# Two gate-quarter loads and a weight split change places at the start of a four-stage transformer kernel

## The reference

```
sh_m, sc_m, gt_m, sh_f, sc_f, gt_f = split(silu(c) @ ada_w[0] + ada_b[0], 6)
h  = rms_norm(x, norm_g[0, 0]) * (1 + sc_m) + sh_m
y  = pool_mixer(h, pool_w, pool_scale)          # 4 groups of 256 columns, windows 2, 4, 8, 16
x  = x + gt_m * rms_norm(y, norm_g[0, 1])       # the "new x"
hf = rms_norm(x, norm_g[0, 2]) * (1 + sc_f) + sh_f
x  = x + gt_f * rms_norm(square(relu(hf @ ffn_w1[0])) @ ffn_w2[0], norm_g[0, 3])
```

## Time and profile before

| | |
|---|---|
| Runs | 972.87, 975.52, 980.09 us |
| Profiled execution | 980.94 us, span 978.9 us |
| TensorE (PE), matmul | busy 957.6 us, 98% of the span |
| VectorE (DVE) | 533.5 us, 54% |
| ScalarE (ACT) | 333.8 us, 34% |
| GpSimd (POOL) | 36.2 us, 4% |
| Chain that ended last | 94% PE, 2% DVE, 2% DMA, 1% ACT |
| Granted TensorE clock, mean | 0.989 of full speed |

### The profile page before, as it was taken

How to read it: one execution, slowest core, us unless ns; L and a number is a source line. 1 busy time by engine, 2 the same in 40 slices (tenths; PEclk the granted TensorE clock), 3 DMA queues, 4 the chain that set the end, 5 groups by cost and what they waited for, 6 DMA issues and landing times.

```text
span 978.9 us, 11447 instructions
## 1 busy us (share of the span) xinstructions
PE 957.6 (98%) x4783; PEld 788.2 (81%) x4783; DVE 533.5 (54%) x598; ACT 333.8 (34%) x437; POOL 36.2 (4%) x70
## 2 busy tenths in 40 slices
PE   6989999999999999999999999999999999999997
PEld 4658888888888888889888888888888888888886
DVE  5586374554355546686667546756445324433444
ACT  5554441431143123353322233543134113412422
POOL 3002000010001000000101000000000000000000
PEclk9899999999999999999999999999999999999999
DMA  9798364344434444414755531254423332233201
GB/s 304 258 338 268 131 226 161 129 157 145 177 129 157 137 151 177 138 44 156 227 183 203 189 108 43 87 194 144 174 91 108 92 124 87 86 92 123 86 22 65
DMA packets 80587, 144.66 MB, mean 148 GB/s; under 512 B 3950, under 2 KB 33746, under 8 KB 80536
## 3 DMA queue, kind: packets, MB, share of 16 engines
q1 hardware_dynamic: 78376, 139.52, 42.5%
q0 software_dynamic: 2160, 4.41, 1.3%
HBM read 141.79 MB, written 2.13 MB: 147 GB/s over the span
## 4 chain that ended last, share of the span: by engine, by line
PE 94%; DVE 2%; DMA 2%; ACT 1%; issue 1%; SPq 0%; DVEq 0%
PE ps L416 30%; PE ps L418 29%; PE ps L417 29%; PE ps L612 2%; DMA win<-in_ada_w_dram 1%; PE ps L662 1%; PE ps L527 1%; DMA xs<-in_x_dram 1%; PE ps L690 0%; PE ps L632 0%; PE ps L445 0%; PE ps L658 0%; DVE bands L1268 0%; DVE y L1150 0%; PE ps L619 0%
## 5 line engine op out<-in xcount | busy, mean ns | idle before, releaser
L1080 DVE TENSOR_TENSOR w_parts<-raw,w_parts 128x2048 fp32r<-128x2048 f32 x81 | 185.6, 2292 | 258.4 <-ACT w_parts L836 258.3
L416 PE MATMUL ps<-in_hi,w_parts 128*128 128x512 f32 (+1 forms) x784 | 290.0, 370 | 0.9 <-DVE in_lo L1161 0.5
L417 PE MATMUL ps<-in_lo,w_parts 128*128 128x512 f32 (+1 forms) x784 | 288.0, 367 | 0.0
L418 PE MATMUL ps<-in_hi,w_parts 128*128 128x512 f32 (+1 forms) x784 | 288.0, 367 | 0.0
L836 ACT ACTIVATE w_parts<-raw 128x2048 fp32r<-128x2048 f32 x81 | 154.7, 1911 | 387.8 <-PE ps L418 386.8
L416 PE MATMUL ps<-w_parts,mid_hi 128*128 128x512 f32 x576 | 224.4, 390 | 0.0
L418 PE MATMUL ps<-w_parts,mid_lo 128*128 128x512 f32 x576 | 224.1, 389 | 0.0
L417 PE MATMUL ps<-w_parts,mid_hi 128*128 128x512 f32 x576 | 224.1, 389 | 0.0
L416 PEld LDWEIGHTS ps<-in_hi,w_parts 128*128 128x128 f32 x784 | 147.7, 188 | 29.3 <-issue 3.3
L418 PEld LDWEIGHTS ps<-in_hi,w_parts 128*128 128x128 f32 x784 | 147.7, 188 | 24.6
L417 PEld LDWEIGHTS ps<-in_lo,w_parts 128*128 128x128 f32 x784 | 147.8, 188 | 24.1
(11 more groups left out here) (152 smaller groups left out, 468.6 us busy)
## 6 DMA issues: line engine op xcount, KB each, us to landing
raw<-in_ffn_w_dram SPq DMA_DIRECT2D x64, 1024.0 KB, 5.2
ada_raw<-in_ada_w_dram SPq DMA_DIRECT2D x56, 512.0 KB, 5.5
raw<-in_conv_in_w_dram SPq DMA_DIRECT2D x16, 512.0 KB, 5.4
raw<-in_ada_w_dram SPq DMA_DIRECT2D x4, 1024.0 KB, 9.7
ada_sum<-in_ada_w_dram SPq DMA_DIRECT2D x4, 1024.0 KB, 12.5
win<-in_ada_w_dram SPq DMA_DIRECT2D x4, 1024.0 KB, 11.9
raw<-in_conv_in_w_dram SPq DMA_DIRECT2D x4, 1024.0 KB, 6.3
raw<-in_conv_out_w_dram SPq DMA_DIRECT2D x4, 1024.0 KB, 5.5
```

Source lines behind the costliest of these rows:

```text
L416: nc.tensor.matmul(o, hi, b_hi, start=start, stop=False)
L417: nc.tensor.matmul(o, hi, b_lo, start=False, stop=False)
L418: return nc.tensor.matmul(o, lo, b_hi, start=False, stop=stop)
L1080: nc.vector.tensor_tensor(w_lo[:, u % W_SLOTS, :], raw[:, u % RAW_SLOTS, :], w_hi[:, u % W_SLOTS, :].bitcast(F32), ALU.subtract).then_inc( ...
```

## The change

SyncE issues all loads up to 11, the four gate quarters among them, ahead of `load(1)`; before, 10 and 11 came behind it. TensorE sums quarter 10 ahead of `pool_group(3)` and quarter 11 right behind it. VectorE copies gate quarters 2 and 3 out earlier; its `split_lo(1)` moves from behind `group_gate(0)` to behind the new x of the second tile; and `first_x(2)` moves behind `first_lo(0)`. ScalarE does `first_hi(0)` ahead of `first_root(2)`; its `split_hi(1)` stays where it is, ahead of the squares of groups 2 and 3. Nothing is added or removed.

```diff
@@ SyncE @@
-            for i in range(2, 10):
+            for i in range(2, PRE_F):
                 load_pre(i)
             load(1)
-            for i in range(10, PRE_F + 6):
+            for i in range(PRE_F, PRE_F + 6):
                 load_pre(i)
             load(2)
@@ TensorE @@
             add_up(9)
             turn_up(4)
+            add_up(10)
             pool_group(3)
+            add_up(11)
             turn_up(5)
-            add_up(10)
-            add_up(11)
             turn_up(6)
             turn_up(7)
@@ ScalarE @@
             first_root(0)
             first_root(1)
             copy_sums(8)
+            first_hi(0)
             first_root(2)
-            first_hi(0)
             copy_first(0, 2)
             first_root(3)
@@ VectorE @@
             group_out(2)
             gate_copy(1)
             group_gate(0)
-            split_lo(1)
+            gate_copy(2)
             group_out(3)
+            gate_copy(3)
             group_gate(1)
-            gate_copy(2)
             dve.wait_ge(y0_sq, NT * GROUPS)
             ...
-            gate_copy(3)
             group_gate(2)
             ...
             group_gate(3)
             first_x(0)
             first_x(1)
-            first_x(2)
+            split_lo(1)
             first_norm(0)
             first_norm(1)
             columns(8)
             first_input(0)
             first_lo(0)
+            first_x(2)
             first_x(3)
             first_norm(2)
             first_norm(3)
```

## The result

The changed kernel takes 980.0 us at the median of 14 runs (979.51 to 983.26), the kernel before 975.51 us at the median of 14 (972.87 to 981.5). The ratio is 1.0051, with a 95% interval of 1.0036 to 1.0066: a loss of 3.5 to 6.4 us, 5.0 at the middle; the medians themselves are 4.5 us apart. The forecast was +2.3 us, at 977.8. Direction, place and range hold; the size is under half of what was measured.

What follows compares the result with a forecast made beforehand. It took the first transposes of both sides to bound the kernel, fed by the load queue and the ScalarE/VectorE chain. New x +0.5, side 0 +0.1, side 1 +1.5 and clock +0.2 gave +2.3 us, 977.8; range 973.2 to 982.3.

Steps and rivals of the forecast that it cites:

- The loads: SyncE's queue: unit 1, now behind loads 10 and 11, lands at 57.4 us instead of 53.5, bounds 56.8 and 58.2.
- So they fill the hole: Loads 10 and 11 take up 2.7 us unused in the load queue at 46 to 50 us.
- Rival 2: Hole not filled: unit 1 lands at 60.1 and the chain is 2.7 us later, +5.0 us, 980.5; chance 0.08.
- ScalarE and the new x: Squares wait behind unit 1's split; the last ends at 62.7, 1.0 us later, and decides narrowly: first_x(0) at 65.6, +0.5.
- the predicted 2 us: VectorE waits about 2 us ahead of group_out(3), for group 3's pool products.
- Side 0: New x, split and two norms end at 72.0; turn_first(0, 0) starts at 72.05, +0.6 us.
- Side 1: First_x(2) behind first_lo(0): side 1 normed at 80.8, TensorE idles 1.5 us, turn_first(1, 0) +2.1 us.
- The clock: Idle TensorE ahead of 72.05 can put the low clock on real work, the transposes: +0.2 us.
- Rival 1: A gain: the split's 2.20 us comes fully off VectorE's chain, 974.9 us; chance 0.15.
- Rival 3: Low clock of 13.0 us or a little more from about 71 us: +6.8 us, 982.3; chance 0.12.
- The base: The profiled execution goes from 980.94 to 983.2; being 5.4 us above the median 975.52, the median goes to 977.8.

Runs made afterwards that it cites:

- single run: The kernel before, unedited, profiled in one execution without the early low clock of 20 to 33 us: span 973.1 us, median 975.13 us.
- early stand-ins: 12 stand-in matmul calls behind add_up(0) and turn_x(3), added to both kernels: 974.63 us on the kernel before, 980.92 us on the changed kernel.
- run 7: Changed kernel with the 12 early stand-in calls, split_hi(1) moved behind the squares of groups 2 and 3: 977.58 us.
- run 5: Changed kernel with 20 more late stand-in calls around turn_up(8): 979.63 us; with split_lo(1), first_x(2) and first_root(2) also moved: 977.64 us.
- run 3: Changed kernel with SyncE's load order of before, load(1) ahead of loads 10 and 11: 980.26 us, ratio 1.005.
- run 4: Changed kernel with split_lo(1) moved behind group_gate(1), into VectorE's wait for the last squares: 980.35 us, ratio 1.0052.
- run 2: Kernel before with only SyncE's load order of the change, loads 10 and 11 ahead of load(1): 981.23 us, ratio 1.0053.
- run 8: Kernel before with early stand-ins, its 6 late calls moved ahead of add_up(13) as 8: 975.34 us; with the 6 kept as well: 974.3 us.
- the last run of the table: Kernel before with 12 early stand-in calls, 8 more in the wait for load 13 and the 6 old ones kept: 974.3 us, ratio 0.998.

## Why the prediction was right in direction and short in size

I set the single run and the changed kernel beside each other, both without the early low clock, and count from `add_up(9)` (47.51 in the single run, 46.80 in the changed kernel):

| | single run | changed | cost so far | predicted |
|---|---|---|---|---|
| unit 1 split | 0.86 | 6.98 | +6.1 | +2.8 |
| sums of squares | 8.07 | 12.32 | +4.3 | +1.0 |
| first_x(0) | 11.36 | 15.12 | +3.8 | +0.5 |
| turn_first(0, 0) | 18.14 | 21.58 | +3.4 | +0.6 |
| turn_first(1, 0) | 25.35 | 30.72 | +5.4 | +2.1, with the clock +2.3 |

- **The loads: the term that was sized wrongly.** "So they fill the hole" took the 2.7 us of one execution for the kernel's. With the low clock of 20 to 33 us sums took 1.93 us, slots came free late and the queue ran dry: the two profiles that have this stretch show a share of 0.36 and 0.42 at 46 to 50 us. Without it the hole is 0.9 us, in the single run and with early stand-ins alike. And unit 1 gets next to nothing even of that. It lands at 53.8, and load 11, last of the three in the single run, at 43.06 + 10.8 = 53.9. So the term that stood in the sum at -2.7 measured -0.1, or +0.6 counted from `add_up(9)`: that is the difference between +2.8 and +6.1, and it runs on almost unchanged to the last row. Load 13 does come 1.1 us earlier (`add_up(13)` at 59.79, in the single run 60.87); why unit 1 has no share in this stays open.
- **What unit 1 pays** for the two loads ahead of it is 11.9 instead of 5.4 us from issue to landing. The Trainium skill (DMA: Bandwidth & Descriptors, "Queues, rings and completion order") has descriptors on each engine consumed in ring order. The trace agrees: 6.5 us for two loads of 1 MB, which at the 348 GB/s of a full stretch take 3.0 us each. Rival 2 had this case nearest, with unit 1 landing late and +5.0, though for another reason.
- **ScalarE and the new x: the path was right.** The last square does decide, not `group_out(3)` or the gates, and run 7 shows the link. Its step was sized by the landing: +3.8 instead of +0.5. The 2.45 us that VectorE waits for group 3 are the predicted 2 us, hidden under the squares.
- **Side 0: +0.6 predicted, +3.4 measured.** The split and the norms are as worked out (61.92 to 67.57 + 0.75: 6.4 us, predicted 6.4). Before it is 5.4, so side 0 costs 1.0. In the single run the first transposes were held not by the norms but by load 13 and stand-ins at 1.2 GHz, 1.4 us behind them; the changed kernel gets there without that, which gives back 1.3. So +3.8 becomes +3.4.
- **Side 1: right.** 8.75 predicted, 8.67 with the clock up (run 5).
- **The clock: too small, and in the wrong relation.** +0.2 was put on as a term of its own; in fact low clock and side 1 lie over each other. In the changed kernel the two are level: TensorE waits 0.18 us for the norm, 9.14 us after the first transposes, and with the low clock taken away (run 5) it is 8.67, the length of side 1's chain by itself. In runs 3 and 4, and with early stand-ins, the low clock is the longer of the two, at 9.96, 9.87 and 9.89 us with no wait at the end, up to 1.3 above side 1's 8.67. That excess over side 1 is the clock's own price.
- **Rival 1, a gain, is out**: VectorE did wait for products and squares. **Rival 3, the long low stretch**, is out in its length, 6.6 us instead of 13; it did fall on the first unit, and begins 3 us ahead of the first transposes instead of 1.
- **The base.** The profiled execution was 5.4 us above the median, and I carried a difference worked out on it over to the median, which belongs to executions without the early stretch. The runs' own times point the same way. Of the 14 runs of each kernel, the upper ones (4 of before, 979.5 to 981.5; 5 of the changed kernel, 981.46 to 983.26) have medians 2.1 us apart, near the forecast of +2.3; the lower ones (up to 976.66, and up to 980.56) have medians 5.5 us apart. The grouping was made afterwards, by time alone, no upper execution of the changed kernel was profiled, and their mean clocks (0.987 to 0.993) are not all as low as those of before, so this is a hint and not shown.

That two halves of the change cost the whole each (runs 2 and 3) is no contradiction: in either the first transposes end up late, by 5.0 and 1.7 us against the single run, and in the second the low clock on the first unit adds 2.8 us.

What stays open is a part of the difference between 6.3 us of loss with early stand-ins and 5.0 without. The 5.0 compares with executions of before of which a quarter are on the upper level; the profiles, counted from `add_up(9)`, are 6.4 and 5.4 apart, and show two parts. From the first transposes to `turn_first(1, 0)` it is 9.89 us with the later low stretch (68.1 to 75.0) and 9.14 without early stand-ins; and in the kernel before, the first transposes come 0.55 us sooner with them. One profile of each doesn't prove either part. Not tried was what sets the place of the low stretch, nor what would be left of the 2.95 us of run 7 without it.

## What to carry to other kernels

Before costing anything against a gap in a profile, ask whether the gap is the kernel's or the execution's: where single runs fall on two levels and the profiled one lies on the rare one, its holes and waits may be smaller in the typical run, and stand at another time: here 0.9 us at 42 to 46 instead of 2.7 at 46 to 50. Look for them at the same instruction, not at the same microsecond. Two loads that were moved ahead of a third in a full queue cost it their full transfer time, and what to look at is what stands in program order behind the wait for it, here eight squares behind a split. Idle time moved next to dense work put the low clock on that work here, and taking away only the low clock showed next to nothing, since a chain of nearly the same length lay beneath it.

## What the runs showed of the hardware

Stand-in matmuls in two gaps of TensorE took away an upper level of 979 to 982 us that 7 of 29 runs of the kernel had; none of 36 runs with them was above 976. The granted clock in such an execution was 0.50 for 13 us, with TensorE busy all the time; small sums and window products didn't bring it back until 33 us. In the changed kernel it was back at 72.0, after 3.6 us of transposes and sums. The Trainium skill (TensorE: Matmul & The Clock Gate, "HAM oscillation — how this bites in real kernels") describes waits for data that make the next tile start throttled. The changed kernel agrees, with 4.01 us of idle followed by 0.50, and the last run of the table, with both gaps filled, kept 0.999. In the single run it fell at 58.3 without a wait that long: TensorE's gaps in the 4 us before were of 0.4 to 0.7 us. The unexpected part is that the price doesn't go by the length of the low stretch. 6.8 us of it, where a sum and stand-ins ran (the single run, 58.3 to 65.1), made the first transposes 1.3 us late (18.1 instead of 16.8 from `add_up(9)`), and 3.4 us of it cost 1.5 us where the first unit's work ran (run 8, 8.75 instead of 7.21 us). Where side 1's longer chain hides most of it, 6.8 us cost 0.5 (the changed kernel) to 1.3 (run 3).
